# Four-tap convolution taken out of PSUM, and the work around it in another order, in a two-block hybrid model on one core

## The reference, cut to what matters

```
def hybrid_layer(x, ...):                                   # first block, twice
    h = rms_norm(x, norm_w)
    aq, ak, av, az, c_glu, cz, dq, dk, dvv, dz, db, da, gates = split(h @ w_in)
    y_a = diff_attention(rope(aq), rope(ak), av, az, ...)
    a, g = split(c_glu); u = a * sigmoid(g)
    u = causal_depthwise_conv(u, dw_w) + dw_b               # 31 taps
    y_c = (silu(layer_norm(u)) * silu(cz)) @ w_conv_out
    qkv = silu(causal_depthwise_conv([dq, dk, dvv], conv_w))  # 4 taps, 3072 channels
    q, k, v = l2_normalize(q), l2_normalize(k), v
    beta = sigmoid(db); g = -exp(a_log) * softplus(da + dt_bias)
    y_d = gated_delta_rule(q, k, v, g, beta) ... @ w_dn_out
    return x + (sigmoid(gates) . [y_a, y_c, y_d]) @ w_out

def second_block(...):                                      # twice
    q = rope(rms_norm(q)); k = rope(rms_norm(k))            # per head
    attn = latent_attention(q, k, v, k_ctx, v_ctx)
    hyena_mix: 3-tap convolution, then a long convolution by Fourier transform
    ...; swiglu
```

## Time and profile before

| | before |
|---|---|
| median of three runs | 2876.27 us |
| the profiled execution | 2872.72 us, its span 2870.9 us |
| PE busy | 2594.4 us, 90% of the span |
| DVE, ACT, POOL busy | 1328.1, 1329.8, 1485.6 us |
| mean granted PE clock | 0.956 of full speed |
| chain that ended last | PE 73%, DVE 13%, ACT 5%, POOL 4%, issue 3% |

### The profile page before, as it was taken

The page is one execution under the profiler, slowest core; times in us unless marked ns, Lnnn a source line. Parts: engine busy times, 40 slices in busy tenths (PEclk is TensorE's granted clock), DMA queues, the critical chain, the costliest instruction groups (busy, mean ns, idle before and its releaser), DMA issues.

```text
span 2870.9 us, 42145 instructions
## 1 busy us (share of the span) xinstructions
PE 2594.4 (90%) x16608; PEld 2222.6 (77%) x16608; DVE 1328.1 (46%) x2212; ACT 1329.8 (46%) x2161; POOL 1485.6 (52%) x858
## 2 busy tenths in 40 slices
PE   6978989888897898998989899998999988898997
PEld 6967878878896687886757676676788867788997
DVE  7976744423588673333537642214100116745213
ACT  5445954445544594444553331234233334444543
POOL 6853855337884485433543122464455545273870
PEclk9998999999998899999989999999999999999999
DMA  5522433334452233324342111223222222134553
GB/s 214 190 103 88 148 136 118 129 125 168 174 182 103 96 140 135 130 103 151 133 146 74 44 56 62 74 88 121 74 88 96 95 103 103 61 131 162 176 181 142
DMA packets 50553, 347.63 MB, mean 121 GB/s; under 512 B 5312, under 2 KB 8640, under 8 KB 8896
## 3 DMA queue, kind: packets, MB, share of 16 engines
q1 hardware_dynamic: 47840, 340.31, 33.0%
q10 hardware_dynamic: 2528, 4.72, 0.5%
HBM read 343.96 MB, written 1.05 MB: 120 GB/s over the span
## 4 chain that ended last, share of the span: by engine, by line
PE 73%; DVE 13%; ACT 5%; POOL 4%; issue 3%; DMA 1%; SPq 0%; ACTq 0%; POOLq 0%; DVEq 0%
PE pg L1669 18%; PE pg L1671 18%; PE pg L1670 18%; POOL ring_lo L592 3%; DVE big L1277 3%; PE pg L1695 2%; PE ps L1916 2%; PE ps L1924 2%; DVE big L1274 1%; PE ps L1922 1%; PE ps L1809 1%; ACT ring_hi L700 1%; PE ps L2058 1%; PE ps L1790 1%; DMA ring<-in_w_stream_dram 1%
## 5 line engine op out<-in xcount | busy, mean ns | idle before, releaser
L592 POOL TENSOR_TENSOR ring_lo<-ring,ring_hi 128x1024 fp32r<-128x1024 f32 (+3 forms) x500 | 1173.2, 2358 | 933.8 <-ACT ring_hi L700 933.4
L1669 PE MATMUL pg<-HH,ring_hi 128*128 128x256 f32 (+1 forms) x3360 | 1078.8, 321 | 41.8 <-issue 17.7
L1670 PE MATMUL pg<-HH,ring_lo 128*128 128x256 f32 (+1 forms) x3360 | 1034.8, 308 | 0.0
L1671 PE MATMUL pg<-HL,ring_hi 128*128 128x256 f32 (+1 forms) x3104 | 962.4, 310 | 0.0
L1669 PEld LDWEIGHTS pg<-HH,ring_hi 128*128 128x128 f32 x3360 | 646.8, 192 | 118.3 <-issue 51.3
L1670 PEld LDWEIGHTS pg<-HH,ring_lo 128*128 128x128 f32 x3360 | 648.0, 193 | 41.0 <-issue 12.6
L1671 PEld LDWEIGHTS pg<-HL,ring_hi 128*128 128x128 f32 x3104 | 598.0, 193 | 31.2
L700 ACT ACTIVATE ring_hi<-ring 128x1024 fp32r<-128x1024 f32 (+6 forms) x564 | 556.2, 1001 | 42.1 <-DMA ring<-in_w_stream_dram 32.0
L710 ACT ACTIVATE take<-pg 128x256 f32<-128x256 f32 (+1 forms) x284 | 120.2, 423 | 472.4 <-PE pg L1671 421.2
L1671 PE MATMUL pg<-big_r,ring_hi 128*128 128x256 f32 (+1 forms) x864 | 276.3, 320 | 0.0
L1669 PE MATMUL pg<-big_r,ring_hi 128*128 128x256 f32 (+1 forms) x736 | 242.7, 330 | 10.4 <-DVE big_r L1618 3.1
(11 more groups left out here) (290 smaller groups left out, 3563.1 us busy)
## 6 DMA issues: line engine op xcount, KB each, us to landing
ring<-in_w_stream_dram SPq DMA_DIRECT2D x320, 1024.0 KB, 4.8
hn<-in_consts_dram ACTq DMA_DIRECT2D x2, 1024.0 KB, 5.2
cst<-in_consts_dram SPq DMA_DIRECT2D x1, 1472.0 KB, 19.5
prm<-in_params_dram SPq DMA_DIRECT2D x1, 1110.0 KB, 7.4
X<-in_xT_dram SPq DMA_DIRECT2D x1, 1024.0 KB, 5.7
X<-in_ctxT_dram ACTq DMA_DIRECT2D x1, 1024.0 KB, 7.9
out_dram<-H ACTq DMA_DIRECT2D x1, 1024.0 KB, 4.8
cst<-in_consts_dram SPq DMA_DIRECT2D x1, 768.0 KB, 16.5
```

Of the source, the lines that this page charges most:

```text
L592: pool.tensor_tensor(ring_lo[:, slot, cols], ring[:, slot, cols], ring_hi[:, place * P:(place + n) * P].bitcast(F32), SUB).then_inc(sem(LO ...
L1669: first = pe.matmul(out, a[0], b[0], start=start, stop=False)
L1670: pe.matmul(out, a[1], b[0], start=False, stop=False)
L1671: return first, pe.matmul(out, a[0], b[1], start=False, stop=stop)
```

## The change

The four-tap convolution no longer has a copy in SBUF. ACT writes the last tap's product from PSUM straight to `DN` (a Copy with a scale per channel, semaphore `dn_first`), and DVE adds the other three taps with SCALAR_TENSOR_TENSOR that read the chunk in `pg` and the running sum in `DN`. The buffer `raw` and its zero columns are gone. A `dn` bank is therefore free for PE when DVE has finished the taps (semaphore `sconv`), not when ACT has read it; `DRAINED` counts the other chunks, and a helper `bank_free` picks the wait.

Around it: the last pair of `conv31` is stretched over the `dn` chunks, 12 of its 31 steps ahead of them and 3 behind each pair from chunk 4 on. Four of the eight rotations go up into the `v` stage, the other four stand at `dn` chunks 1 to 4. The layer norm moves from chunk 9 to chunk 18, and its root is Ln and Exp written to PSUM in place. The squares of q go to the free half of `H`; the head norms of q and k move behind the last `dn` chunk; their roots, and that of the delta rule's output, stay in PSUM and DVE reads them there. The gate sums move to columns 256 to 303 of bank 3 of `ps`; their second half (`delta_log`, `delta_decay`) runs in the first steps of the attention loop. In the second block one rotation stands behind each of the first three chunks and two behind the fourth, and the scores wait only for the rotations that they read.

```
-        ROPE_AT = [8, 10, 11, 12, 13, 14, 15, 16]
-        DQ_AT = 18
-        DK_AT = 22
-        ROPES_AFTER = [[0], [1, 2], [3, 4], []]
+        ROPES_V = 4
+        CONV_EARLY = 12
+        LN_AT = 18
+        MGQ = H[:, :, T:2 * T]
+        ROPES_AFTER = [[0], [1], [2], [3, 4]]
...
+            def bank_free(j):
+                if j >= 4:
+                    name, l, i = ORDER[j - 4]
+                    if name == "dn":
+                        pe.wait_ge(sem("sconv"), 24 * l + i + 1)
+                    else:
+                        pe.wait_ge(sem("drained"), DRAINED[name, l, i])
...
-                    drain(CHUNK["dn", l, j], raw[:, j % 4, SHORT_K - 1:])
+                    act.activation(DN[:, j, :], ready(CHUNK["dn", l, j])[:, 0:T], ACT.Copy,
+                                   scale=PR("dn_conv_w", ...)).then_inc(sem("dn_first"), 1)
+                    if j % 2 and j > 1:
+                        dn_silu(j - 3)
+                        dn_silu(j - 2)
...
-                            ins = dve.tensor_scalar(DN[:, k, :], raw[:, k % 4, 0:T], PR("dn_conv_w", w), None, MUL)
+                        ins = dve.scalar_tensor_tensor(DN[:, k, t:T], pg[:, CHUNK["dn", l, k] % 4, 0:T - t], PR("dn_conv_w", w),
+                                                       DN[:, k, t:T], MUL, ADD)
...
# DVE's stream
-                for m in range(0, KD, 2):
-                    conv31(l, m)
+                for m in range(0, KD - 2, 2):
+                    all_of(conv31(l, m))
+                for jj in range(ROPES_V):
+                    rope1(jj)
+                last = conv31(l, KD - 2)
+                for t in range(CONV_EARLY):
+                    next(last)
+                for j in range(0, 24, 2):
+                    if j == LN_AT:
+                        all_of(last)
+                        dve.wait_ge(sem("ln_mean"), l + 1)
+                        dve.scalar_tensor_tensor(CV, rep(ps[:, 0, 0:T], KD), -1.0 / D, CV, MUL, ADD)...
+                    sconv(l, j)
+                    if j < 8 - ROPES_V:
+                        rope1(ROPES_V + j)
+                        rope1(ROPES_V + j + 1)
+                    else:
+                        for t in range(3):
+                            next(last, None)
+                dve.wait_ge(sem("ln_rms"), l + 1)
+                dve.tensor_tensor(CV, CV, rep(ps[:, 1, 0:T], KD), MUL).then_inc(sem("ln_normed"), 1)
...
# PE's delta_gates
+                pe.wait_ge(sem("ln_normed"), l + 1)
+                head_norm(HN_BASE1(l) + DQ_N, 2048, MGQ)
                 fill([("cz", l, 0)])
-                pe.wait_ge(sem("hn_rms"), HN_BASE1(l) + DK_N + 1)
+                pe.wait_ge(sem("hn_done"), HN_BASE1(l) + DQ_N + 1)
+                head_norm(HN_BASE1(l) + DK_N, 2048)
+                fill([("cz", l, m) for m in range(1, EARLY_CZ // 2)] + mods(l, "gates"))
+                fill([("cz", l, 2)])
+                pe.wait_ge(sem("hn_done"), HN_BASE1(l) + DK_N + 1)
                 ... the 48 gate matmuls, now into ps[:, 3, 256:288] ...
+                fill([("cz", l, 3)])
...
# second block, PE
-                pe.wait_ge(sem("rope"), ROPE2[l] + 5)
...
+                        pe.wait_ge(sem("rope"), ROPE2[l] + 2 + steps[k][0] // 2)
                         attention2_scores(i, steps[k])
+                    if k == LAG:
+                        pe.wait_ge(sem("rope"), ROPE2[l] + 5)
```

More of the change, by code:

```diff
@@ L846, in delta_gates @@
                 drain_fill([("cz", l, 0)])
-                act.wait_ge(sem("ba_ready"), l + 1)
-                both = ps[:, 0, 0:32].rearrange("p (c n) -> p c n", c=NT)
-                act.activation(BETA, both[:, :, 0:HEADS], ACT.Sigmoid).then_inc(sem("beta"), 1)
+                hn_root(HN_BASE1(l) + DK_N, 2048, 1.0)
                 act.activation(EXA, PR("dn_a_log", l * HEADS, HEADS), ACT.Exp).then_inc(sem("exp_a"), 1)
+                drain_fill([("cz", l, m) for m in range(1, EARLY_CZ // 2)])
+                drain_fill(mods(l, "gates"))
+                drain_fill([("cz", l, 2)])
+                drain_fill([("cz", l, 3)])
                 act.wait_ge(sem("abs_a"), l + 1)
+                act.activation(BETA, BA[:, :, 0:HEADS], ACT.Sigmoid).then_inc(sem("beta"), 1)
                 act.activation(B1, B1, ACT.Exp, scale=-1.0).then_inc(sem("exp_abs"), 1)
@@ L854, in delta_gates, with delta_decay @@
                 act.activation(B2, B1, ACT.Ln, bias=1.0).then_inc(sem("ln_abs"), 1)
-                drain_fill([("cz", l, m) for m in range(1, EARLY_CZ // 2)])
-                drain_fill(mods(l, "gates"))
+            def delta_decay(l):
                 act.wait_ge(sem("gc_ready"), l + 1)
-                act.activation(BEG, ps[:, 1, 0:16].rearrange("p (c h) -> p c h", c=NT), ACT.Exp)\
-                    .then_inc(sem("exp_gc"), 1)
-                drain_fill([("cz", l, m) for m in range(EARLY_CZ // 2, EARLY_CZ)])
+                act.activation(BEG, GCS, ACT.Exp).then_inc(sem("exp_gc"), 1)
             def delta(l, u):
@@ L944, in _ @@
-                    if j == LN_AT:
+                    if j == LN_AT + 3:
                         act.wait_ge(sem("ln_ss"), l + 1)
[L946 to L951, removed]
@@ L962, in _ @@
+                act.wait_ge(sem("dn_silu"), 24 * l + 16)
+                hn_square(DN[:, 8:16, :])
+                act.wait_ge(sem("ln_normed"), l + 1)
+                for m in range(KD):
+                    act.activation(CV[:, m, :], CV[:, m, :], ACT.Silu, bias=PR("conv_ln_b", l * KD + m),
+                                   scale=PR("conv_ln_w", l * KD + m)).then_inc(sem("ln_silu"), 1)
                 dn_silu(22)
                 dn_silu(23)
+                hn_root(HN_BASE1(l) + DQ_N, 2048, 1.0)
@@ L1871, in delta_gates, with delta_decay @@
                         t = slice(c * P, (c + 1) * P)
-                        first, ins = parts(ps[:, 0, c * 16:(c + 1) * 16], (HH[:, k, t], HL[:, k, t]), (WB_HI[:, a], WB_LO[:, a]),
+                        first, ins = parts(BA[:, c, :], (HH[:, k, t], HL[:, k, t]), (WB_HI[:, a], WB_LO[:, a]),
                                            k == 0, k == KD - 1)
                 ins.then_inc(sem("ba_ready"), 1)
-                fill([("cz", l, m) for m in range(1, EARLY_CZ // 2)] + mods(l, "gates"))
+                fill([("cz", l, 3)])
+            def delta_decay(l):
                 pe.wait_ge(sem("g_done"), l + 1)
                 for c in range(NT):
-                    ins = pe.matmul(ps[:, 1, c * HEADS:(c + 1) * HEADS], C("until"), G[:, c, :], start=True, stop=True)
+                    ins = pe.matmul(GCS[:, c, :], C("until"), G[:, c, :], start=True, stop=True)
                 ins.then_inc(sem("gc_ready"), 1)
-                fill([("cz", l, m) for m in range(EARLY_CZ // 2, EARLY_CZ)])
-                pe.wait_ge(sem("gates_done"), l + 1)
             def delta(l, u):
```

153 lines of the change are left out of this document (74 added, 79 removed).

## The result

The changed kernel took 2851.05 us (median of four runs, 2850.57 to 2856.22), the kernel before on the same chip 2875.3. The ratio is 0.992 (95% interval 0.9908 to 0.9932): 24 us faster. The forecast was 2855, from 2851.0 for the profiled execution; the one profiled after took 2850.85 (span 2848.6).

The account below looks back on a forecast made before the run. DVE, its SBUF-only instructions held by POOL, was taken to pace PE in mid-`dn`. Two layers' -14.4 and the second block's -7.3 make -21.7: 2872.72 to 2851.0 profiled, median 3.55 higher, about 2855 us; range 2834 to 2878.

Parts of the forecast that it names:

- the 1.5 set aside for the loop: Attention loop, per layer: `delta_log` ahead of the second step on DVE, possibly held; costs 0 to 3.0 us, 1.5 taken.
- Rival D: `dn` stage: taps reading PSUM are held by POOL too, twice a pair; slower, 2939 us; chance 0.03.
- two inputs in SBUF: DVE in `dn`: POOL holds instructions with two SBUF inputs, not those reading PSUM; worst step 2.63 us.
- The estimated 65 ns per tap: DVE taps: the skill's rule against the change, 62 cycles more for PSUM reads; 1.6 us in all.
- The stage: `dn` of layer 0: PE paces chunks 4 to 17; end moves from 267.1 to 236.9, gain 30.2 us.
- the mean: Layer norm at chunk 18: 16 matmuls cost 3.6 us at full clock, 5.8 after idling; 4.7 taken.
- the rotation's wait: Early `dn`, after three chunks and a rotation: PE waits 4.1 us for the next rotation's space.
- The tail: Last `dn` chunk to the load before the first attention Exp: one chain of 55.6 us, was 34.1; loss 21.5.
- The two norm sums: Head norms behind the last `dn` chunk: sums for k on PE cost half of 9.1, 4.6 us.
- The middle between both clocks: Tail, `cz` 2, 48 gate matmuls and `cz` 3: 10.7 us at full clock, 20.7 at half; 15.7 taken.
- -7.2 each: Each first-block layer: -30.2 for `dn`, +21.5 behind it, +1.5 for `delta_log`; bounds -18.7 to +8.8 us.
- The second block: Spread rotations start attention earlier, -3.8 us in layer 0 and -3.5 in layer 1; -7.3 taken, ends -2 and -10.

## Why the prediction was right

The total was right (2855 against 2851), and so was the mechanism: the taps are no longer stretched, PE sets the pace of the stage, and the tail gives much of the gain back. The terms were less exact than the total, and partly cancelled: the tail ran 2.7 over, and the 1.5 set aside for the loop was not needed. At the load ahead of the first attention Exp, layer 0 was 6.6 us ahead and layer 1 had gained 7.3, where stage and tail make 8.7 in the sum. That the total came out within 4 us of the median is in part luck.

- **The hold.** In the kernel before 42 of the 192 tap instructions take over 0.6 us. All 42 run beside a `ring_lo` subtraction of POOL and end 0.15 to 0.29 us behind its end; of the 150 others 8 run beside one. In the changed kernel 102 of the 144 taps do, and none is stretched. The stretch came back with the copy, and was shorter with shorter POOL instructions. Rival D had no place. The prediction's words for what is held, two inputs in SBUF, are too narrow: 26 of the 42 are TENSOR_SCALARs, which read one tile and a column of `prm`. What these runs show held are instructions that read SBUF alone. Nor is it the number of instructions: without a hold eight of them would take an estimated 3.1 us per pair (2 x 0.34 and 2.45), under PE's 5.64. The estimated 65 ns per tap that the Trainium skill ("VectorE: DVE Perf Modes", section "The TRN2 errata — SBUF-src ops pay a fixed extra latency per instruction") would have added do not show: 472 ns is the median of both kernels' taps.
- **The stage.** `dn` begins at 147.8 (148.3 forecast), PE goes through chunks 4 to 17 without a wait, the last chunk ends at 236.3 (236.9). The prediction sets this beside 267.1, where `cz` 0 ends in the kernel before; the last `dn` chunk ended at 264.3, so the gain is 28.0, and would have been 27.4 by its own end. The tail is off by the same 2.8 the other way, and the sum is not touched. Within the stage the mean took 6.6 where 4.7 was taken, nearly all at half clock behind its wait (0.52 granted from 208.9 to 215.0); the rotation's wait was 2.6 for 4.1.
- **The tail.** The load ahead of the first attention Exp on ACT answers the earlier trace rows:

```profile
294.59 1.28 ACT L846 ACT_TABLE_LOAD   x1
```

  It stands 58.3 behind the last chunk, for 55.6. Before it stood 36.9 behind it (34.1 behind `cz` 0), so the loss is 21.4, and 18.7 was forecast by that count. The two norm sums took 5.6 and 5.8 for 4.6 (the q sums stand beside the Silus). Of the 48 gate matmuls, which begin at 276.6 and end at 284.1, the first part ran at the full clock and the rest at half. Both windows of PE, columns as in the earlier trace rows:

```profile
276.60:279.40 2.80, 2.80 (x28) 2.80 (x26) 0.00 (x0) 1.33 (x2) 2.80 (x3) 1.00 0.03 9
279.80:284.00 4.20, 4.20 (x21) 4.20 (x21) 0.00 (x0) 0.00 (x0) 3.04 (x2) 0.50 0.00 0
```

  The middle between both clocks was the right choice for them; what ran over are the two `cz` chunks around them, mostly at half: the three together took 17.8 for 15.7. (At half clock they make 10.26 and 2 x 5.64, so 21.5 and not 20.7; the middle would have been 16.1.)
- **The loop.** 1.5 was taken for a held instruction in `delta_log`, and this term was not there: those instructions took 0.17 to 0.25 us. PE waits 4.3 in an early step for ACT, which has the decay's Exp and its table load in between, but that only uses up PE's lead at the first scores (11.1): the gain is 6.6 at the first Exp and 6.5 to 7.0 from the fifth step to 380 us. It shrinks to 5.0 between 384 and 402, where the same matmuls ran at a lower clock than in the kernel before (columns as in the earlier trace rows; before, then after):

```profile
382.00:402.00 20.00, 13.25 (x51) 8.08 (x52) 1.22 (x2) 12.47 (x15) 8.26 (x5) 0.83 0.32 105
```

```profile
375.20:397.00 21.80, 14.95 (x51) 8.71 (x52) 1.26 (x2) 12.48 (x15) 8.47 (x5) 0.77 0.26 96
```

  Layer 1 loses 0.1 there. So the size came out by luck.
- **What was not in the sum.** Between 580 and 650 us layer 0 gained another 3.0. Of these 2.2 came where the same matmuls ran at a higher clock (before, then after):

```profile
568.70:596.80 28.10, 23.83 (x170) 20.87 (x169) 8.95 (x12) 14.09 (x24) 11.01 (x6) 0.88 0.39 150
```

```profile
563.60:589.50 25.90, 21.25 (x171) 18.37 (x171) 9.00 (x12) 14.12 (x24) 10.31 (x6) 1.00 0.45 163
```

  Layer 1 has no such gain, so I count it as chance. 0.7 stand at a modulation on DVE. Layer 0 ended at -8.0 and layer 1 at -7.0 (forecast -7.2 each), and another 0.8 came up to the second block.
- **The second block.** In the two traces the attention's start moves by 5.2 and 2.3 more than the work ahead of it, and 6.5 of that last, for 7.3. The start of layer 0 answers the earlier trace rows:

```profile
1575.28 0.68 DVE L1550 TENSOR_REDUCE at_m<-ps 128x1 f32<-128x512 f32 x1
```

  What stands last there is now ACT, no longer a rope, as PE's waits from 1540 to 1580 us show against the earlier trace rows. In layer 1, from 2400 to 2436, ropes still hold PE for 5.5 of the 7.0, and so its start moved by 2.3 for 3.5:

```profile
PE ps L2076 <- ACT at_buf L1031: 4.8, 1, 4.8
PE ps L1846 <- DVE big L1437: 1.0, 1, 1.0
```

```profile
PE ps L1846 <- DVE big L1437: 5.5, 2, 4.2
PE ps L2076 <- ACT at_buf L1031: 4.1, 1, 4.1
```

What the prediction did not see: it priced the gain of the stage (30) and the loss of the tail (21) as one trade, and did not ask whether the first needs the second. It does not. With the old order the taps alone gave 35 us, because the stage became 18 shorter per layer and the tail hardly changed.

What stays open: how the 16 to 20 us that the new order costs divide. Starting the long convolution earlier gives 8 to 12 of them back; the place of the gates gives nothing here and 9.5 elsewhere; the late norms cost the tail some 17 per layer, but the run that moved them inside lost 20 in the stage, so what they cost in the end is not shown.

## What to carry to other kernels

Where an engine is held by another one's instruction, move the operand out of their common reach first, and measure that alone: the freed time may make a new order needless. A table of busy shares shows that ACT has room inside a stage, but a root of 6.4 us in one piece needs a place where the weights ahead and the taps behind it can wait; moving roots, squares and rotations by a few chunks made 22 to 27 us here (2834.8 to 2808.1 by the medians, 44.6 to 67.1 by the differences to the kernel before). Work that is taken out of a full stage and put behind it is not hidden, it is the path.

## What was not expected of the hardware

Cut into quarters, POOL's instruction took 0.80 to 0.88 us where a quarter of 2.45 is 0.61. The kernel before has `ring_lo` subtractions of several lengths: the medians are 0.47 us for 128 columns, 0.74 for 256, 1.29 for 512 and 2.40 for 1024. So some 0.2 us (an estimate from these differences) belong to the instruction and not to its columns. What a quarter took beyond 0.74 (median 0.90 with held taps beside it, 0.73 in the later run without) goes with the taps; that DVE holds POOL in turn would fit, and is not shown. Cutting gained 12 us where taps were held and lost 12 where they were not and `cz` was cut as well.
